# Four more expert steps of two slots in the mLSTM heads of the second half

## The reference

```python
def peer(h, w_q, sub_keys, expert_u, expert_v):
    q = jnp.einsum('bsd,dq->bsq', h, w_q).reshape(b, s_len, PEER_HEADS, 2, PEER_HALF)
    scores = jnp.einsum('bshpc,hpnc->bshpn', q, sub_keys)
    top_s, top_i = lax.top_k(scores, PEER_TOPK)
    ...
    best_s, best_pos = lax.top_k(cand_s, PEER_TOPK)
    best_i = jnp.take_along_axis(cand_i, best_pos, axis=-1)
    gate = jax.nn.softmax(best_s, axis=-1)
    ...
    u = jnp.take(expert_u, ib, axis=0)
    act = jax.nn.gelu(jnp.einsum('td,tkd->tk', xb, u), approximate=False)
    vv = jnp.take(expert_v, ib, axis=0)
    y = jnp.einsum('tk,tkd->td', gb * act, vv)
```

## Time and profile before

| | |
|---|---|
| median of 3 runs | 2930.36 us (2926.49 to 2931.91) |
| the profiled execution's own time | 2931.76 us |
| its span, first to last instruction | 2930.0 us |
| TensorE, mean granted clock | 0.876 |
| VectorE busy | 1826.2 us, 62% of the span |
| TensorE busy | 2313.1 us, 79% |
| ScalarE busy | 632.2 us, 22% |
| GpSimd busy | 790.1 us, 27% |
| DMA | 798.24 MB, mean 272 GB/s |
| table loads on ScalarE | 44, mean 1283 ns |

### The profile page before, as it was taken

The page is one execution under the profiler, slowest core; times in us unless marked ns, Lnnn a source line. Parts: engine busy times, 40 slices in busy tenths (PEclk is TensorE's granted clock), DMA queues, the critical chain, the costliest instruction groups (busy, mean ns, idle before and its releaser), DMA issues. The chain is left out here.

```text
span 2930.0 us, 26186 instructions
## 1 busy us (share of the span) xinstructions
PE 2313.1 (79%) x9012; PEld 1706.8 (58%) x9012; DVE 1826.2 (62%) x3679; ACT 632.2 (22%) x1424; POOL 790.1 (27%) x544
## 2 busy tenths in 40 slices
PE   8999999999889999899899779987534455555454
PEld 7887588887668888666788666766411122122111
DVE  1101335413245897765777784857888888888886
ACT  1001502101431301245121024711111111111110
POOL 0000000000000244321443431312266555546552
PEclk9999599999979999999999888979768777777777
DMA  4433137753223799962899964725499999999996
GB/s 174 153 145 121 24 131 285 274 187 129 72 85 132 281 390 411 361 236 83 365 422 421 416 254 157 268 84 231 173 398 421 405 422 421 421 396 421 421 421 284
DMA packets 114659, 798.24 MB, mean 272 GB/s; under 512 B 13280, under 2 KB 16480, under 8 KB 19040
## 3 DMA queue, kind: packets, MB, share of 16 engines
q0 software_dynamic: 74880, 541.10, 45.4%
q1 hardware_dynamic: 39648, 255.47, 23.2%
HBM read 790.23 MB, written 6.29 MB: 272 GB/s over the span
## 5 line engine op out<-in xcount | busy, mean ns | idle before, releaser
L482 PE MATMUL PS<-reg,ring 128*128 128x256 f32 x6016 | 1364.2, 388 | 38.3 <-DVE reg L1273 13.5
L482 PEld LDWEIGHTS PS<-reg,ring 128*128 128x128 f32 x6016 | 1157.0, 194 | 226.3 <-issue 50.0
L433 POOL DMA_INDIRECT uv<-in_expert_uv,experts x322 | 527.2, 1637 | 1958.2 <-DVE experts L1168 946.3
L1210 DVE SCALAR_TENSOR_TENSOR acc<-uv,coef,acc 128x1024 f32<-128x1024 f32 x261 | 335.3, 1285 | 10.0 <-DVE coef L1195 0.8
L461 PE MATMUL PS<-uv,diag 128*128 128x512 f32 x228 | 154.0, 826 | 237.3 <-ACT diag L852 237.3
L1183 DVE CUSTOM_DVE_ANT_0 uv<-uv,h_tok 128x1024 f32<-128x1024 f32 x226 | 269.3, 1219 | 53.8 <-DMA uv<-in_expert_uv,experts 53.7
L461 PEld LDWEIGHTS PS<-uv,diag 128*128 128x128 f32 x228 | 59.0, 274 | 335.8 <-issue 335.8
L859 ACT ACTIVATE acts<-dots 128x2 f32<-128x2 f32 (+1 forms) x192 | 39.1, 204 | 993.4 <-DVE dots L1183 899.3
L461 PE MATMUL PS<-reg,diag 128*128 128x512 f32 x228 | 163.7, 874 | 106.0 <-ACT diag L852 106.0
L461 PEld LDWEIGHTS PS<-reg,diag 128*128 128x128 f32 x228 | 60.8, 281 | 207.2 <-issue 207.2
L433 POOL DMA_INDIRECT reg<-in_expert_uv,experts x114 | 141.9, 1245 | 88.7 <-PE PS L461 61.9
(11 more groups left out here) (241 smaller groups left out, 2354.1 us busy)
## 6 DMA issues: line engine op xcount, KB each, us to landing
ring<-in_weights SPq DMA_DIRECT2D x228, 1024.0 KB, 6.8
uv<-in_expert_uv,experts POOLq DMA_INDIRECT x322, 14.1
reg<-in_x_t SPq DMA_DIRECT2D x2, 1024.0 KB, 5.8
kv_half<-reg SPq DMA_DIRECT2D x1, 2048.0 KB, 11.0
reg<-in_sub_t SPq DMA_DIRECT2D x2, 1024.0 KB, 4.7
x_tokens<-reg SPq DMA_DIRECT2D x2, 1024.0 KB, 4.0
toep<-in_rel_pad SPq DMA_DIRECT2D x16, 128.0 KB, 3.2
reg<-kv_half SPq DMA_DIRECT2D x1, 2048.0 KB, 15.0
```

The lines of the kernel that those rows point to most:

```text
L433: gp.indirect_dma_start(UV[r], None, a["expert_uv_2"], bass.IndirectOffsetOnAxis(ap=experts[:, e % 256:e % 256 + 1], axis=0))\
L482: mm = pe.matmul(out_tile(n, t), w[:, t * P:(t + 1) * P], mv, start=first and k == 0, stop=last and k == KT - 1)
L1210: dve.scalar_tensor_tensor(acc[:, :], v, c, acc[:, :], ALU.mult, ALU.add).then_inc(acc_done, 1)
```

## The change

TensorE, ScalarE and VectorE each take one more step of their generator behind each of the four mLSTM heads of the second half. So the second half holds 104 steps, and the tail begins at step 104, slot 208. `EARLY` counts the four new steps too; it is false before (100 > 120) and after (104 > 120), so the routings stay where their steps are.

```diff
--- before.py
+++ after.py
@@ -129,7 +129,7 @@
     _held[_r] = _e
 
 TICKS = [int(hf == 1 and (kind, i) not in ((V1, 3), (WO, 3), (DN, 15), (V2, 0), (V2, 1), (WO2, 3))) for hf, kind, i in SEQ]
-EARLY = sum(TICKS) + 4 > GROUP_OF[15 * TOPK]
+EARLY = sum(TICKS) + 4 + NML > GROUP_OF[15 * TOPK]
 
 
 def build(nc, a, out):
@@ -690,6 +690,8 @@
                     if e + 1 < NML:
                         scores(e + 1)
                     values(e)
+                    if hf:
+                        next(experts_pe)
                 pe.wait_ge(ml_y, NML * (hf + 1))
 
             def half(hf):
@@ -1076,6 +1078,8 @@
                     if e >= 2:
                         act.wait_ge(ml_y, mb + e - 1)
                     act.activation(scr[:, 2 + e % 2, :], PS[:, 4 + e % 2, T:2 * T], ACT.Abs).then_inc(ml_abs, 1)
+                    if hf:
+                        next(experts_act)
                 act.wait_ge(ml_y, NML * (hf + 1))
                 for m in range(8):
                     if m >= 4:
@@ -1609,6 +1613,8 @@
                     dve.reciprocal(den, den).then_inc(ml_rec, 1)
                     dve.wait_ge(ml_rec, mb + e + 1)
                     dve.tensor_tensor(mixed(4 + e), PS[:, 4 + e % 2, 0:T], den, ALU.mult).then_inc(ml_y, 1)
+                    if hf:
+                        next(experts_dve)
                 head_inverse(hf, 3)
                 for m in range(8):
                     head_scale(hf, 3, m, mixed(m), col("g_out_sb", m))
```

## The result

| | before | changed |
|---|---|---|
| median, of 13 runs each | 2930.56 us (2926.0 to 2932.06) | 2938.09 us (2933.55 to 2945.83) |
| the profiled execution's own time | 2931.76 us | 2933.55 us |
| its span | 2930.0 us | 2931.7 us |
| mean granted clock of TensorE | 0.876 | 0.877 |
| table loads at the gelus' line | 44 | 47, and 2 more at line 1069 |

The 44 loads of the table of the kernel before are those of the gelus' line alone; in all there are 135. The change adds the five that were forecast.

The account below looks back on a forecast made before the run. The prediction took DMA, at 2.49 us a slot, to bound the tail, and a chain across engines the heads. Its terms, 24.4 - 1.3 - 17.6 = +5.5 us, gave 2936.0 us, range 2928 to 2945.

Parts of the forecast that it names:

- The steps in the heads: Second half's mLSTM heads: a head with a step takes 12.92 us instead of 6.12; squares start 24.4 us later.
- TensorE off the chain: In the heads, TensorE's values of a head end 2.5 us before ScalarE asks for them, so TensorE adds nothing.
- The gathers cost nothing in the heads: Each added step's two gathers go into a DMA share of 0.05 and land well before their dots: no cost.
- WO2 keeps its time: Layer behind the heads: it keeps its 3 steps, each four indices later; predicted difference up to its root 0.
- PQ: Routing moves from the fifth PQ step to the first and covers a longer wait: 1.3 us earlier.
- A first PQ wait of about zero: Sign expected in the changed profile: VectorE's first wait in PQ, 2.14 us before, is about zero.
- The start of the tail: From slot 208 on: issued right behind ScalarE's last copy, slots 2.49 us apart; slot 219 lands 17.6 us earlier.
- The reason given for the tail's gain: Tail's start: of 17.6 us, four fewer slots give 10.0; the rest is DMA time wasted by the slow start.
- Rival 1: TensorE stays at its lower clock behind the heads, slowing WO2: 2942 us with two more slow groups; chance 0.13.
- rival 2: Heads: a change of table costs twice its row, five loads 1.28 us more each, 2942 us; chance 0.03.
- Rival 3: Heads hide ScalarE's part and step 3, so only VectorE's time counts: -5.9 us, 2924.5 us; chance 0.05.
- Rival 4: Tail loses all eight slots and its slow start, 10.0 us more gain: -4.5 us, 2926 us; chance 0.07.

Follow-up runs that it names:

- no_table: The changed kernel with tanh for gelu in steps 89 to 92, so five table loads fewer; 2928.72 us in one execution.
- late_gelu: The changed kernel with ScalarE's part of each added step one head later, the last behind the root; 2926.81 us, ratio 0.998 to 0.9998 to the kernel before.
- two_heads: The changed kernel with added steps behind heads 0 and 1 only; 2935.11 us in one execution.
- late_write: The changed kernel with SyncE's 1 MB write of the second half's tokens held until TensorE has done four tail slots; 2939.74 us.

## Why the prediction was right

By its own steps:

- **The steps in the heads**: 12.92 us a head, measured 12.99 and 12.80; step 1 and 2 at +12.9 and +25.8 us, measured 12.99 and 25.8 (1943.78); step 3 at +35.5, measured 35.3; the squares +24.4, measured +24.3. This held because the order of instructions on both engines gave the chain, and each link had a row of the same operation. no_table and late_gelu confirm the links one by one: what was ScalarE's 1.7 us in a head, what was VectorE's 4.99.
- **TensorE off the chain**, with 2.5 us of cover: right (2.9), and two_heads shows what happened without it (+2.7).
- **The gathers cost nothing in the heads**: right, VectorE has no wait for DMA there. WO2 keeps its time: 48.6 against 48.7.
- **PQ** -1.3: measured -1.2. The account behind it named two waits; the trace has more. Before, VectorE waits 2.14 us behind the first step and again behind the one that follows the routing. With the routing in the first step the first of these is gone and the second stands behind the second step, with waits of 0.86 us behind all later ones but the last:

```profile
2049.26 0.29 DVE L1640 MAX8 reg<-reg 128x8 f32<-128x128 f32 x1 [2.14 <-ACT reg L1094]
```

  What moved with the routing cancels, and 2.14 - 0.87 is left, as forecast. "A first PQ wait of about zero" holds behind the first step; the wait ahead of the first top list stays (5.10 us, before 5.27).
- **The start of the tail**, -17.6: measured -16.6. This is the term that was mis-sized. Its parts: issue 0.3 us after the last copy (0.4 taken), the rate of 2.49 us a slot (from slot 208 to 225 17 slots in 42.1 us, 2.48), and the landing of slot 208, for which I took the 6.7 us of a quiet queue. It took 8.1, because SyncE's write of the tokens starts at the same moment; late_write makes it 5.7. That is 1.4 us, and with the earlier issue and the rate about the 1.0 that is missing.
- **The reason given for the tail's gain** was "Four slots are 10.0 us; the rest is DMA time that the tail's slow start wasted". The landing times bear it out: 10.0 and 6.1 us. What it leaves out is that the slow start goes step by step, at VectorE's 5.41 us, so that it says nothing of what one step is worth: three steps take 16.2 us off and reach the floor, the fourth 0.35. The prediction took the four as one block, so I saw no reason to ask whether fewer would do.
- **Rivals.** Rival 1 falls by WO2's first groups, rival 2 by no_table. Rival 3 was no rival as the change stood, but late_gelu, which moves ScalarE's calls, gets half of it (2.9 us under the kernel before, where rival 3 had 5.9). Rival 4: the tail didn't get the further 10 us; it is at its floor.

The sum by the stretches, +6.6, is 1.1 us over the forecast: 1.0 in the tail's start, 0.1 elsewhere. The medians' +7.5 us lies at 0.26%, just past the edge of 0.2% at which the forecast of +5.5 stood; the chances of 0.47 within and 0.46 slower said as much. Between the stretches' 6.6 and the medians' 7.5 and 8.8 us one or two microseconds are in no stretch; the intervals (6.4 to 10.8 and 5.0 to 10.8 us) don't tell them from nothing. What stays open is the part ahead of the change: the place of step 0 lies between 1917.0 and 1925.5 us in the 13 profiles, with the same program up to there. 3.5 us of this are the clock in which the scores of head 1 run; for the rest, up to the copy of `b_cols` (1901.9 to 1907.2), no run shows a cause.

## What to carry to other kernels

A step moved out of a bound stage gains only until the next bound is reached, so ask for each moved piece separately what it gains and what it costs; here the first three were worth 5.4 us each and the fourth 0.35, and the four together cost 24.3 us where they were put. Look for the places where the engine that does the work waits for others (here the roots and the first tiles of a layer), and put the in-order partner's part behind what the chain needs from it: three steps were then free. An idle DMA and a busy VectorE can be one loss and not two: the gathers wait for buffers that VectorE frees. And a landing time measured in a quiet queue doesn't hold where another queue starts its write at the same moment.

## What the runs showed of the hardware

- A change of table and back cost 1.67 us on the chain of a head, less than its two rows of 1.28, since ScalarE would have waited for VectorE for 0.91 us of it (no_table). No further cost beside the rows showed.
- 24 idle matmuls held the granted clock at 1.00 through a gap in which it was otherwise 0.50, and the head means behind it were 1.7 us faster; the clock fell again (0.62) ahead of the next layer. PQ and the stretch to the end were 0.4 and 0.8 us longer in this run, and its single execution (2934.46 us) doesn't prove a gain for the whole.
- The same program up to step 0 ran the scores of head 1 in 3.36 us in 8 of 13 profiles and in 1.78 in 5, which made 3.5 us between executions.
- A gather into the tail lands 5.7 us after its issue with nothing beside it and 8.1 us with a 1 MB write; the difference of 2.4 us is what 1 MB takes at the full rate (2.49).
